# Multiplications of zeros ahead of x in other shapes: strides, offsets, a broadcast, and half widths

## What is computed

```python
def swiglu(h, w13, w2):
    gate, up = jnp.split(h @ w13, 2, axis=-1)
    return (jax.nn.silu(gate) * up) @ w2

# first_block: for l in range(DEPTH)
x = x + 0.5 * swiglu(rms_norm(x, ffn1_norm[l]), ffn1_w13[l], ffn1_w2[l])
h = rms_norm(x, mix_norm[l])
# l = 0: a gated linear recurrence, l = 1: stick-breaking attention
x = x + 0.5 * swiglu(rms_norm(x, ffn2_norm[l]), ffn2_w13[l], ffn2_w2[l])

# second_block: Fourier mixing with neighbourhood attention, an MLP with squared relu,
# then multi-scale pooling and a second MLP; gains, shifts and gates come from c and ctx
```

## Time and profile before

| | us |
|---|---|
| median of 2 runs | 1479.85 (1479.02 to 1480.67) |
| the profiled execution's span | 1477.2 |
| PE busy in it | 1466.8 (99%) |
| DVE busy | 1240.4 (84%) |
| ACT busy | 832.9 (56%) |
| POOL busy | 117.0 (8%) |

### The profile page before, as it was taken

How to read it: one execution, slowest core, us unless ns; L and a number is a source line. 1 busy time by engine, 2 the same in 40 slices (tenths; PEclk the granted TensorE clock), 3 DMA queues, 4 the chain that set the end, 5 groups by cost and what they waited for, 6 DMA issues and landing times.

```text
span 1477.2 us, 23156 instructions
## 1 busy us (share of the span) xinstructions
PE 1466.8 (99%) x8772; PEld 1291.5 (87%) x8772; DVE 1240.4 (84%) x1742; ACT 832.9 (56%) x1220; POOL 117.0 (8%) x71
## 2 busy tenths in 40 slices
PE   9999999999999999999999999999999999999999
PEld 8888899988888898888779888887789988999888
DVE  7999998989998879999777988875677898787864
ACT  6554668655456645556765454654665455565452
POOL 0013100001311102111000111100000121000110
PEclk9999999999999999999999999999999999999999
DMA  7666754656675647667233877643235588346660
GB/s 276 253 243 254 273 213 158 229 199 235 245 265 194 230 162 285 243 248 257 86 142 119 300 255 265 244 167 143 80 143 209 197 307 299 129 150 234 243 229 29
DMA packets 44703, 311.41 MB, mean 211 GB/s; under 512 B 5760, under 2 KB 6016, under 8 KB 7488
## 3 DMA queue, kind: packets, MB, share of 16 engines
q1 hardware_dynamic: 42192, 303.33, 56.0%
q0 software_dynamic: 1840, 5.73, 1.3%
q10 hardware_dynamic: 576, 1.05, 0.2%
HBM read 308.98 MB, written 1.05 MB: 210 GB/s over the span
## 4 chain that ended last, share of the span: by engine, by line
PE 87%; DVE 8%; ACT 3%; issue 2%; DMA 1%; SPq 0%; DVEq 0%; ACTq 0%
PE psum L2142 18%; PE psum L2153 10%; PE psum L2177 7%; PE psum L2180 7%; PE psum L2043 7%; PE psum L2181 7%; PE psum L2050 7%; PE psum L2049 7%; PE psum L2393 3%; PE psum L2398 3%; PE psum L2399 3%; DVE w_lo L1156 3%; DVE buf L1165 1%; DVE buf L1379 1%; PE psum L2190 1%
## 5 line engine op out<-in xcount | busy, mean ns | idle before, releaser
L1156 DVE TENSOR_TENSOR w_lo<-raw,w_hi 128x1024 fp32r<-128x1024 f32 x478 | 590.8, 1253 | 68.1 <-ACT w_hi L565 67.8
L565 ACT ACTIVATE w_hi<-raw 128x1024 fp32r<-128x1024 f32 x477 | 484.4, 1047 | 90.7 <-PE psum L2153 35.4
L2142 PE MATMUL psum<-u,w_hi 128*128 128x512 f32 x1376 | 325.9, 389 | 0.0
L2142 PEld LDWEIGHTS psum<-u,w_hi 128*128 128x128 f32 x1376 | 258.3, 188 | 53.6
L2043 PE MATMUL psum<-u,w_hi 128*128 128x256 f32 (+1 forms) x872 | 252.5, 290 | 1.3 <-ACT buf L908 0.9
L2050 PE MATMUL psum<-u,w_lo 128*128 128x256 f32 (+1 forms) x872 | 246.4, 283 | 0.0
L2049 PE MATMUL psum<-u,w_hi 128*128 128x256 f32 (+1 forms) x872 | 246.3, 282 | 0.0
L2177 PE MATMUL psum<-w_hi,hid_hi 128*128 128x512 f32 x528 | 206.8, 392 | 0.3 <-issue 0.2
L2180 PE MATMUL psum<-w_hi,hid_lo 128*128 128x512 f32 x528 | 206.5, 391 | 0.0
L2181 PE MATMUL psum<-w_lo,hid_hi 128*128 128x512 f32 x528 | 205.5, 389 | 0.0
L2153 PEld LDWEIGHTS psum<-u,w_lo 128*128 128x128 f32 x1376 | 176.4, 191 | 6.7
(11 more groups left out here) (307 smaller groups left out, 1722.6 us busy)
## 6 DMA issues: line engine op xcount, KB each, us to landing
raw<-stream SPq DMA_DIRECT2D x287, 1024.0 KB, 4.8
buf<-tab POOLq DMA_DIRECT2D x2, 768.0 KB, 4.9
raw<-stream SPq DMA_DIRECT2D x2, 512.0 KB, 5.7
x<-x_in SPq DMA_DIRECT2D x2, 512.0 KB, 6.1
buf<-stream POOLq DMA_DIRECT2D x1, 1024.0 KB, 5.1
buf<-ctx_in POOLq DMA_DIRECT2D x1, 1024.0 KB, 7.5
buf<-poolmat POOLq DMA_DIRECT2D x1, 1024.0 KB, 5.1
out<-x ACTq DMA_DIRECT2D x4, 256.0 KB, 2.0
```

The costliest lines, as they stand in the source:

```text
L565: sc.activation(w_hi[:, u], raw[:, u], ACT.Copy).then_inc(S.hi_ready, 1)
L1156: ve.tensor_tensor(w_lo[:, u], raw[:, u], w_hi[:, u].bitcast(F32), ALU.subtract).then_inc(S.lo_ready, 1)
L2142: ins = te.matmul(bank2(bank), w_hi[:, at + k * P:at + (k + 1) * P], both[:, k, :], start=k == 0, stop=False, skip_group_check=True)
```

## The change

The zeros now lie in the whole of two tiles, `hid_hi` and `hid_lo`, each set by a memset of its own, and PE waits for both. Every multiplication takes its moving operand from `hid_hi` and its stationary one from `hid_lo`. `busy` becomes `warm`, which chooses the width (512 or 256 columns), the step and the offset of either operand (in elements of four bytes; step 0 reads one column 128 times), and one or two PSUM banks. Ahead of the wait for x there are now 19 groups, 82 multiplications of 512 columns and 63 of 256, and four more of 512 behind it. Nothing else differs; lines below the new memset stand one line further down.

```diff
-            ve.memset(zeros.bitcast(F32), 0.0).then_inc(S.zeros_set, 1)
+            ve.memset(hid_hi_t[:, :].bitcast(F32), 0.0).then_inc(S.zeros_set, 1)
+            ve.memset(hid_lo_t[:, :].bitcast(F32), 0.0).then_inc(S.zeros_set, 1)
...
-            def busy(count):
-
-                for _ in range(count):
-                    te.matmul(psum[:, 0, :], zeros[:, 0:P], zeros, start=True, stop=True, skip_group_check=True)
-
-            pe.wait_ge(S.zeros_set, 1)
-            busy(18)
+            def warm(count, columns=512, m_step=1, m_at=0, w_step=1, w_at=0, banks=1):
+
+                moving = hid_hi_t[:, m_at:m_at + columns * m_step:m_step]
+                if w_step:
+                    stationary = hid_lo_t[:, w_at:w_at + P * w_step:w_step]
+                else:
+                    stationary = hid_lo_t[:, w_at:w_at + 1].broadcast_to([P, P])
+                for n in range(count):
+                    te.matmul(psum[:, n % banks, 0:columns], stationary, moving, start=True, stop=True, skip_group_check=True)
+
+            pe.wait_ge(S.zeros_set, 2)
+            warm(16)
+            warm(6)
+            warm(6, w_step=2)
+            warm(6, w_step=4)
+            warm(6, w_at=4)
+            warm(6, w_at=8)
+            warm(6, w_at=64)
+            warm(6, w_step=0)
+            warm(6, m_step=2)
+            warm(6, banks=2)
+            warm(9, columns=256)
+            warm(9, columns=256, w_step=2)
+            warm(9, columns=256, w_step=2, m_at=4)
+            warm(9, columns=256, w_step=4)
+            warm(9, columns=256, w_step=0)
+            warm(9, columns=256, m_step=2)
+            warm(9, columns=256, w_step=2, banks=2)
+            warm(6, w_step=2, m_at=4)
+            warm(6, w_step=2, m_at=2)
             pe.wait_ge(S.x_front_in, 16)
-            busy(4)
+            warm(4)
             swiglu("ffn0", "start")
```

## The result

The changed kernel takes 1505.5 us (median of two runs, 1505.32 and 1505.74) against 1479.85 us: a ratio of 1.0175, interval 1.0146 to 1.0205. Four further runs, beside 19 of the kernel before, gave 1505.1 us and 1.0170 (1.0153 to 1.0187). It is 25 to 26 us longer; the forecast was 22.

The account below looks back on a forecast made before the run. The prediction took PE's gapless queue to bound the kernel: ffn0 begins 22.8 us later, 0.8 us comes back, so 22.0 us is added to 1479.85 us, giving 1502 us. The range was 1499 to 1507 us, at 82%.

Parts of the forecast that it names:

- The bound: From 8.62 us on, PE's queue has almost no slack, so a delay at its head should arrive at the end.
- What comes back: PE's earlier waits for operands, 0.5 us at 8.62 to 14.85 us and 0.3 us at 135 us, vanish: 0.8 us together.
- The memset of 1024 columns: DVE's opening: each larger memset takes 911 ns, two take 1.82 us instead of 0.485, so PE starts 1.34 us later.
- The counts and the paces: Zeros before x: 82 of 512 columns and 63 of 256 at 0.227 and 0.1193 us, so ffn0 begins at 31.4 us.
- The rival of a hidden delay: DVE sets ffn0's end, so its lead of 22 us pays the delay back: near 1480 us; chance 5%.
- groups with a step at another pace: Sign of error among the zeros: strided groups would show a pace other than 0.227 and 0.119 us a matmul.
- the sum: PE's head: start, longer first steps and the zeros make 30.47 us, then four more, so ffn0 begins at 31.4 us.
- The other end is no cost; I take nothing: Strided zeros: steps 2 and 4 charged nothing; bounds were 3.6 us for stationary loads, 2.4 us for moving step 2.
- the mechanism among its rivals: The 16-byte line rule charges the 15 matmuls at step 4: 0.9 us at twice the load, 1503 us; chance 25%.
- I take the same seven at the longer step: First zeros: seven at 0.447 us, 1.54 us above the later pace; bounds none, or all 16, 2.0 us more.
- The start: PE's first multiplication by zeros, behind both memsets, was put at 2.79 us, 1.34 us later than before.
- Offsets alone ... I charge nothing: Zeros whose operands begin 4, 8 or 64 columns in: like the slices every product takes, so 0 us.

Follow-up runs that it names:

- e4: Changed kernel's counts and widths, all but the first 16 and last 4 multiplications with the moving operand at step 2, everything else at step 1; 1523.5 us, 1.0297.
- e1: Changed kernel's counts of 512 and 256 columns, with both operands at step 1, offset 0 and one bank throughout; 1502.0 us, 1.0152.
- e2: Kernel before with only the two larger memsets, the wait for both and the stationary operand from the other tile; 18 and 4 multiplications kept; 1480.5 us, 1.0002.
- e6: Changed kernel's zeros replaced by groups at more steps and offsets, with 512-column unit-step groups between to keep the clock up; only steps read, no total time given.
- e5: Changed kernel's zeros replaced by groups trying steps of either operand one by one at 256 and 128 columns; only steps read, no total time given.
- e3: Changed kernel with no multiplications by zeros at all, memsets and both waits kept; 1480.8 us, 1.0007 against the kernel before.
- e7: Changed kernel's zeros replaced by 24 of 512 columns, 100 of 128, 40 of 512, 60 of 128 with stationary step 8, 40 of 512; no total time given.

## Why the prediction came out as it did

**What held.** The bound: PE is one string without slack behind 8.62 us, and a delay at its head arrives at the end. Heads that were 1.8, 23.0, 27.3 and 45.8 us late (memsets alone, unit steps, the change, step 2 everywhere) ended 0.9, 22.1, 26.3 and 44.9 us late; the changed kernel's second profile adds 1.0 us to this by a late transfer at 244 us. What comes back was put at 0.8 us and is 0.9, for the most part at the two places named: 0.5 us up to the third unit, 0.3 at the first "down". The memset of 1024 columns was put at 911 ns and takes 0.91 us. The counts and the paces of 0.227 and 0.119 us gave the first product at 31.4 us, and with unit steps it stands at 31.66. The rival of a hidden delay fell with the earlier trace rows, as argued, and with e4.

**What failed.** The forecast had named groups with a step at another pace as a sign of being wrong, and they came at another pace. The first product stood at 35.90 us, 4.5 us later than the sum. By terms:

- "The other end is no cost; I take nothing", for the moving operand at step 2. It was the other end: 2.70 - 6 x 0.228 = 1.3 us for 512 columns and 2.03 - 9 x 0.119 = 1.0 us for 256. The bound I had beside it was 2.4 us. The reason given, that a load at the present rate is hidden, speaks of the stationary operand only; for the moving one I had no row, and no ground to prefer the lower end.
- The stationary operand at step 4 under 256 columns: 2.11 - 9 x 0.119 = 1.0 us. The forecast had the mechanism among its rivals at 0.9 us, and gave it one chance in four.
- "I take the same seven at the longer step": ten came. With the same opening the runs had seven (e1), ten (the change, twice) and eleven (e2 and e4), at 0.2 us each, so this is scatter from execution to execution, and no property of the change. 0.6 us here.
- The start: 3.06 us and not 2.79. DVE begins 0.11 us later, and the second memset 0.16 us behind the first. 0.27 us.
- "Offsets alone ... I charge nothing": of 512 columns the groups from offsets 4 and 8 and those with the stationary operand at steps 2 and 4 take 0.233 and not 0.227, and some others begin with a few steps of about 0.23 that don't last (two banks in e6). About 0.3 us in all, found as a remainder: 35.90 - 31.66 = 4.24 us against e1, less 2.3, 1.0 and three more at the longer step.

Together 2.3 + 1.0 + 0.6 + 0.3 + 0.3 = 4.5 us. The time is off by less, 3.7 us (1505.5 against 1479.85 + 22.0). Some 0.1 us more came back than forecast. The rest is chance: the 2.65 us that were to stay between span and median set the median of two runs against the span of the quicker one, and with the change the same difference is 2.0 us (1505.5 less 1503.5). The range, up to 1507 us, held one strided cost and nine more zeros at the longer step; two strided costs and three such zeros came. So the time lies inside it partly by luck, and the predicted 1502 us is the time of the kernel with unit steps.

**The rule on lines.** By the Trainium skill, SBUF — State Buffer, part "SBUF cachelines", a read needs two hits on a line of 16 bytes for full rate. For the stationary operand the runs agree. 128 columns touch 32, 64, 96 and 128 lines at steps 1, 2, 3 and 4, and 128 at every wider one; the loads come at 0.111, 0.118 and 0.173 us (e5) and 0.234 (step 4, the changed kernel), and at 0.229, 0.229 and 0.241 for steps 5, 6 and 8 (e6). Worked out from these, a load takes about 1.82 ns a line and not less than 0.11 us. For the moving operand under 256 columns they differ: step 2 has two hits to a line and is doubled (0.224 us), and step 4 has one and costs hardly more (0.233). The measurement decides. That the array takes two neighbouring elements at a time would fit these numbers, but not the 0.110 us of 128 columns at step 8; it is argued, not shown.

**Another version.** None of the runs beats the kernel before. The zeros save PE about 2 us at the start of ffn0 (e3's trace); the medians differ by 0.9 us, which is not clear of their scatter. More zeros are a plain loss, and a head that is 1.8 us longer (e2) can't be told from none by the time.

## What to carry to other kernels

In a kernel whose matrix engine has no gaps, as here, work put ahead of it is paid in full at the end, whatever leads the other engines gain meanwhile; only waits that were there before come back. Where the matrix engine reads float32, keep the moving operand at unit step (or broadcast it): steps 2, 3 and 4 doubled the time of a matmul of 256 columns, and step 2 that of one of 512. The stationary operand may be at step 2 for next to nothing. At step 4 it doubled a matmul of 256 columns, while under 512 steps 4 and 8 cost 3% and 8% (0.234 and 0.244 against 0.227 us), since the load then takes little longer than the matmul that covers it.

## What the runs showed of the hardware that I had not expected

- A moving operand at step 0 is as quick as at step 1: 0.111 us for 256 columns (0.120 at unit step). A stationary one at step 0 came at 0.114 in the same run and at 0.120 in the changed kernel.
- Multiplications can lower the clock, too. PE was without a gap by the table's busy time in e7, yet among the 60 of 128 columns with the stationary operand at step 8 the granted clock went from 1.00 to 0.50, and the dense group behind began at the lower level. The 60 themselves don't show it: they come at 0.240 us on either side of the fall, so a load at step 8 takes the same time at both levels.
- Up to the first rise of the clock the column of the granted clock reads 1.00 although the steps of 0.427 us show the lower level: 3.06 to 7.43 us in the changed kernel. There the steps are to be trusted, not the column.
- A stationary operand that begins four columns into a tile takes 0.233 us and not 0.227 for 512 columns, and does so for all of 24 in a row (e6); from offset 64 it is 0.227 (the changed kernel). Why is open.
